# A seventeenth place for expert weights, with the tenants of its region moved

## The reference

```python
x = x + gt1 * (merged @ w_out[l])
h = rms_norm(x, norm2_g[l]) * (1.0 + sc2) + sh2
x = x + gt2 * hier_moe(h, ...)
return rms_norm(x, final_norm_g)
# hier_moe, for each of 4 groups of 8 experts:
hid = silu(einsum('td,edf->tef', hf, w1[gi])) * einsum('td,edf->tef', hf, w3[gi])
out = out + einsum('tef,efd->td', hid * combine[:, gi, :, None], w2[gi])
```

## Time and profile before

| | us |
|---|---|
| median of three runs | 686.97 |
| lowest, highest | 686.06, 691.97 |
| the profiled execution | 687.41 |
| its span, first to last instruction | 685.6 |

### The profile page before, as it was taken

The page is one execution under the profiler, slowest core; times in us unless marked ns, Lnnn a source line. Parts: engine busy times, 40 slices in busy tenths (PEclk is TensorE's granted clock), DMA queues, the critical chain, the costliest instruction groups (busy, mean ns, idle before and its releaser), DMA issues.

```text
span 685.6 us, 12601 instructions
## 1 busy us (share of the span) xinstructions
PE 661.1 (96%) x5274; PEld 531.1 (77%) x5274; DVE 428.0 (62%) x723; ACT 267.3 (39%) x375; POOL 71.4 (10%) x70
## 2 busy tenths in 40 slices
PE   8999999999999999999999999999999999999893
PEld 7999999998777778999989997676666666665441
DVE  4756988987777789978999686735242122121226
ACT  3346655548773524347353324231232212121102
POOL 0001000000004524200000000001111111111111
PEclk9999999999999999999999999999999999999997
DMA  8997454455334433356999989989999999999992
GB/s 362 422 377 255 176 184 145 164 184 185 123 123 141 167 124 123 123 174 228 388 398 394 344 320 421 376 309 405 411 395 419 420 421 419 419 418 419 420 362 83
DMA packets 31194, 201.22 MB, mean 293 GB/s; under 512 B 5047, under 2 KB 5431, under 8 KB 7970
## 3 DMA queue, kind: packets, MB, share of 16 engines
q1 hardware_dynamic: 27378, 193.27, 72.1%
q0 software_dynamic: 3760, 7.14, 2.8%
HBM read 195.35 MB, written 10.75 MB: 301 GB/s over the span
## 4 chain that ended last, share of the span: by engine, by line
PE 77%; DMA 9%; DVE 8%; SPq 2%; ACT 2%; issue 2%; DVEq 0%; ACTq 0%
PE ps L1555 75%; DMA ring<-in_expert_pieces 4%; DMA r_v<-in_pieces 4%; DVE ring_rounded L928 3%; SPq L451 1%; PE ps L1699 1%; DVE r_ct L1193 1%; PE ps L1991 1%; DVE r_v L1193 1%; ACT ring_rounded L638 1%; DMA r_xs<-in_x_t 1%; DVE r_xs_rounded L1214 0%; DVE r_kq L1157 0%; SPq L471 0%; DVE r_kq L1151 0%
## 5 line engine op out<-in xcount | busy, mean ns | idle before, releaser
L928 DVE TENSOR_TENSOR ring_rounded<-ring,ring_rounded 128x2048 fp32r<-128x2048 f32 x60 | 136.5, 2290 | 20.2 <-ACT ring_rounded L638 19.7
L1555 PE MATMUL ps<-hT_rounded,ring_rounded 128*128 128x256 f32 x832 | 148.1, 284 | 1.1 <-ACT hT_rounded L652 1.1
L1555 PEld LDWEIGHTS ps<-hT_rounded,ring_rounded 128*128 128x128 f32 x832 | 127.9, 191 | 4.4 <-issue 3.3
L638 ACT CAST ring_rounded<-ring 128x2048 fp32r<-128x2048 f32 x60 | 113.8, 1903 | 30.7 <-PE ps L1555 27.6
L1555 PE MATMUL ps<-ring_rounded,hT_rounded 128*128 128x512 f32 x352 | 111.2, 393 | 0.9 <-DVE r_bt_rounded L1243 0.9
L1555 PE MATMUL ps<-x_sb_rounded,ring_rounded 128*128 128x256 f32 x416 | 94.9, 283 | 0.0
L1555 PEld LDWEIGHTS ps<-x_sb_rounded,ring_rounded 128*128 128x128 f32 x416 | 76.5, 191 | 0.7
L1555 PEld LDWEIGHTS ps<-ring_rounded,hT_rounded 128*128 128x128 f32 x352 | 65.0, 188 | 15.3 <-issue 1.7
L852 ACT ACTIVATE sq<-ps 128x128 f32<-128x128 f32 x32 | 8.9, 277 | 141.3 <-PE ps L1555 141.3
L1438 DVE TENSOR_TENSOR r_st<-ps,r_kq 128x512 f32<-128x512 f32 x32 | 22.1, 692 | 64.9 <-PE ps L1555 64.9
L597 POOL DMA_INDIRECT y_rows<-r_st,r_btm x29 | 28.5, 984 | 317.6 <-DVE r_st L1438 311.5
(11 more groups left out here) (333 smaller groups left out, 1002.0 us busy)
## 6 DMA issues: line engine op xcount, KB each, us to landing
ring<-in_pieces SPq DMA_DIRECT2D x62, 1024.0 KB, 5.0
ring<-in_expert_pieces SPq DMA_DIRECT2D x48, 1024.0 KB, 16.2
r_z<-in_expert_pieces SPq DMA_DIRECT2D x12, 1024.0 KB, 11.7
r_xs<-in_expert_pieces SPq DMA_DIRECT2D x12, 1024.0 KB, 13.0
r_v<-in_pieces SPq DMA_DIRECT2D x8, 1024.0 KB, 8.3
r_ct<-in_pieces SPq DMA_DIRECT2D x8, 1024.0 KB, 6.7
g_sb<-in_expert_pieces SPq DMA_DIRECT2D x6, 1024.0 KB, 13.1
r_st<-in_expert_pieces SPq DMA_DIRECT2D x6, 1024.0 KB, 13.0
```

Of the source, the lines that this page charges most:

```text
L638: nc.scalar.copy(high_of(p_), slot_of(p_)).then_inc(hi_ok, 1)
L928: nc.vector.tensor_tensor(low_of(p_), slot_of(p_), high_of(p_).bitcast(F32), ALU.subtract).then_inc(lo_ok, 1)
L1555: return nc.tensor.matmul(o, l, r, start=start, stop=stop)
```

## The change

`MOE_SLOTS` is 17. The seventeenth place (number 16) is all of `r_kq`. Piece 16 is loaded into it behind pieces 12 and 13, once all four products of the first residual are added (`x2_done`) and the gate's bias has landed. From there the order of places has one more member, so each later piece goes to the place that was free one piece earlier in the list. The tenants of the region move:

- `gt2_two` and `c_half` to the upper 1024 columns of `r_st`. SP loads the bias there behind piece 6, after the merged halves were taken; ScalarE waits for the fourth merged half before it writes `c_half`.
- the three work areas of the search to constants in `par` that nothing reads any more; the search runs after expert 2's output (it was expert 1's), its ranks after expert 3's (2's).
- `fng` to the place whose last piece is used first among the last: place 12, `r_bt`, free after expert 26. POOL loads it behind the scatter of expert 27 (it was 8).
- the pieces of the loop for further windows to places 11, 13 and 14 (they were 2, 3 and 4).

`s_wr` becomes the counter of place 16 too, with a new name.

```diff
-MOE_SLOTS = 16
+MOE_SLOTS = 17
...
+SPARE = [s_ for s_ in range(2, MOE_SLOTS) if max(j for j in range(3 * E) if MOE_SLOT[j] == s_) < 3 * EARLY_E]
+NORM_SLOT = min(SPARE, key=lambda s_: max(j for j in range(3 * E) if MOE_SLOT[j] == s_))
+NORM_FREE = max(j for j in range(3 * E) if MOE_SLOT[j] == NORM_SLOT) // 3
+X_SLOTS = [s_ for s_ in SPARE if s_ != NORM_SLOT][:3]
...
-        gt2_two = r_q[:, 0:CW]
-        c_half = r_q[:, CW:2 * CW].rearrange("p (k n) -> p k n", n=W)
+        gt2_two = r_st[:, 3072:3072 + CW]
+        c_half = r_st[:, 3072 + CW:4096].rearrange("p (k n) -> p k n", n=W)
...
-                     r_xs[:, 2048:4096]] + ring_slot[:6] + [r_bt[:], view(hT, "p k t -> p (k t)")] + ring_slot[6:]
+                     r_xs[:, 2048:4096]] + ring_slot[:6] + [r_bt[:], view(hT, "p k t -> p (k t)")] + ring_slot[6:] + [r_kq[:]]
...
-        fng = r_k[:, 0:D]
+        fng = moe_slots[NORM_SLOT][:, 0:D]
...
-        jt = r_k[:, 0:3 * JOBS * E].rearrange("p (a b) -> p a b", b=E)
...
+        of_job, tmp_j, tmp_k = (par[:, PAR[n][0]:PAR[n][0] + JOBS * E].rearrange("p (a b) -> p a b", b=E)
+                                for n in ("same", "after", "inch"))
...
+        moe_full = [sem(f"moe_full{i}") for i in range(MOE_SLOTS - len(EARLY) - 1)] + early_full + [s_wr_then_moe]
+        full_ahead = [0] * (MOE_SLOTS - len(EARLY) - 1) + [1] * len(EARLY) + [3]
...
-                    for h in range(2):
-                        sp.dma_start(gt2_two[h * W:(h + 1) * W], gate_bias[h].partition_broadcast(W)).then_inc(s_wr, 16)
...
             for n in range(6):
                 piece_used(sp, RING_FREED[n][1])
                 load_moe(6 + n)
+                if n == 0:
+                    sp.wait_ge(s_wr_then_moe, 16)
+                    for h in range(2):
+                        unit_taken(sp, ("ob", 1), h)
+                    for h in range(2):
+                        sp.dma_start(gt2_two[h * W:(h + 1) * W], gate_bias[h].partition_broadcast(W)).then_inc(s_wr_then_moe, 16)
...
             load_moe(13)
+            sp.wait_ge(x2_done, 2 * TT)
+            sp.wait_ge(s_wr_then_moe, 48)
+            load_moe(16)
...
-                if e == 8:
-                    pool.wait_ge(jobs_ok, 1)
+                if e == NORM_FREE + 1:
+                    for done in (up_read, up_full, down_full):
+                        pool.wait_ge(done, NORM_FREE + 1)
                     pool.dma_start(fng, final_norm_g.partition_broadcast(P)).then_inc(s_crow_fng, 16)
...
+            act.wait_ge(m_full, 4)
             nc.scalar.copy(c_half, over(col("c", 0, 8), W)).then_inc(c_done, 1)
...
-            dve.wait_ge(s_wr, 48)
+            dve.wait_ge(s_wr_then_moe, 16)
...
             dve.wait_ge(gate_read, len(GATE_ROWS))
+            dve.wait_ge(s_wr_then_moe, 48)
             nc.vector.tensor_tensor(gt2_two, ps[GATE_BANK][:], gt2_two, ALU.add).then_inc(gate_ok, 1)
...
-                if e == 1:
+                if e == 2:
                     extra_windows()
...
-                if e == 2:
+                if e == 3:
                     ranks_of_extra_windows()
```

More of the change, by code:

```diff
@@ L306, in trunk @@
         start_row_read, mod_ok, x_sqrt_crow = (sem(n) for n in "start_then_row_read mod_ok x_sqrt_then_c_rows".split())
-        moe_full = [sem(f"moe_full{i}") for i in range(MOE_SLOTS - len(EARLY))] + [
-            sem(f"early_then_moe_full{i}") for i in range(len(EARLY))]
-        early_full = moe_full[MOE_SLOTS - len(EARLY):]
+        early_full = [sem(f"early_then_moe_full{i}") for i in range(len(EARLY))]
         hi_ok, lo_ok, half_read, ob_read, ada_read, up_read, gate_read, gate_ok, h_full, h_hi, m_full, m_hi, ob_hi, oa_hi, h_lo = (
@@ L325, in trunk @@
         fin_sqrt, fin_scaled, out_ready = (sem(n) for n in "fin_sqrt fin_scaled out_ready".split())
-        s_xT, s_x, s_small, s_par, s_const, s_ones, s_wr, s_crow_fng, s_gate = (sem(n) for n in "s_xT s_x s_small s_par s_const s_ones s_wr s_crow_fng s_gate".split())
+        s_xT, s_x, s_small, s_par, s_const, s_ones, s_wr_then_moe, s_crow_fng, s_gate = (sem(n) for n in "s_xT s_x s_small s_par s_const s_ones s_wr_then_moe s_crow_fng s_gate".split())
+        moe_full = [sem(f"moe_full{i}") for i in range(MOE_SLOTS - len(EARLY) - 1)] + early_full + [s_wr_then_moe]
+        full_ahead = [0] * (MOE_SLOTS - len(EARLY) - 1) + [1] * len(EARLY) + [3]
         s_pool = sem("s_pool_chain")
@@ L422, in moe_loaded @@
         def moe_loaded(eng, j):
-            eng.wait_ge(moe_full[MOE_SLOT[j]], 16 * (moe_turn(j) + 1 + (MOE_SLOT[j] >= MOE_SLOTS - len(EARLY))))
+            eng.wait_ge(moe_full[MOE_SLOT[j]], 16 * (moe_turn(j) + 1 + full_ahead[MOE_SLOT[j]]))
         def col(name, i=0, n=1):
@@ L482, in _ @@
                         unit_taken(sp, ("oa", 1), h)
-                    sp.dma_start(r_btm[:, 0:KD * 36 + 36], router_w).then_inc(s_wr, 16)
+                    sp.dma_start(r_btm[:, 0:KD * 36 + 36], router_w).then_inc(s_wr_then_moe, 16)
                     load_moe(3)
@@ L541, in _ @@
                     for h in range(3):
-                        sp.dma_start(moe_slots[2 + h], expert_pieces[e * 3 + h]).then_inc(x_loaded, 16)
+                        sp.dma_start(moe_slots[X_SLOTS[h]], expert_pieces[e * 3 + h]).then_inc(x_loaded, 16)
                     sp.wait_ge(x_added, j)
@@ L1366, in _ @@
             nth = over(count0[:, 0:JOBS], E)
-            of_job, tmp_j, tmp_k = (jt[:, i * JOBS:(i + 1) * JOBS] for i in range(3))
             def extra_windows():
@@ L2065, in _ @@
                     pe.wait_ge(x_taken, j)
-                    up([up_half(2 + r) for r in range(2)], lambda r: r or pe.wait_ge(x_loaded, j * 48), ps[0], x_rows, up_read, x_up)
+                    up([up_half(X_SLOTS[r]) for r in range(2)], lambda r: r or pe.wait_ge(x_loaded, j * 48), ps[0], x_rows, up_read, x_up)
                     pe.wait_ge(x_hid, j)
@@ L2069, in _ @@
                     pe.wait_ge(x_back, j)
-                    down(down_w(4), hidT[:, 0], ps[2], x_down)
+                    down(down_w(X_SLOTS[2]), hidT[:, 0], ps[2], x_down)
                     pe.wait_ge(x_weighted, j * 2)
```

## The result

| | before | after |
|---|---|---|
| median, us (14 runs each) | 687.03 | 682.51 |
| lowest, highest | 685.64, 691.97 | 681.55, 685.61 |
| profiled execution | 687.41 | 682.08 |

The ratio is 0.9939, with a 95% interval of 0.9926 to 0.9952: 4.2 us (3.3 to 5.1) faster. The forecast was 683.7 with a range of 682.5 to 686.1. The median lies inside by 0.01 us, which is luck as far as the range goes: the interval of the ratio reaches to both sides of that edge. The change of 0.6% is under the 1% that was called no change.

What follows compares the result with a forecast made beforehand. TensorE was taken to bound the kernel, waiting for expert weights near the end. TensorE's gain of 3.8 us less 0.2 for late reads gave -3.6 us: 683.7 us, range 682.5 to 686.1.

Steps and rivals of the forecast that it cites:

- The place: Expert weight stream: piece 16 fills unused transfer time from 444 to 460 us, so later pieces land 2.5 us earlier.
- The norm's row: Final norm's broadcast, moved behind expert 27's scatter: pieces awaited from 625 to 648 us come another 1.25 us earlier.
- TensorE's waits: End of expert stage: 4.06 us lost waiting for weights; 3.8 us gained, 0.3 us of waiting left.
- The search: Search for experts with over 64 rows, one expert later: TensorE 0.5 us earlier in mid stage, costed at nothing.
- The end: POOL's reads of scattered rows overlap the last weights 1.3 us more; 0.2 us loss taken, 1.3 upper bound.
- The other tenants: Gate bias, copies, search work areas and extra-window slots at new addresses: hidden, 0, at most 0.1 us either way.
- more gain: Expert stage: a fuller queue moves bytes better, waits vanish, the search's 0.5 us counts: -4.6, 682.8 us; chance 0.13.
- the gap does not take the piece: From 444 to 460 us other pieces are pushed back, only the norm's row gains: -1.3, 686.1 us; chance 0.09.
- the reads cost the full 1.3 us: Kernel's end: last weights and four reads collide for all 1.3 us: -2.5, 684.9 us; chance 0.15.
- nothing is visible: Whole kernel: an unseen wait eats the gain, time stays 687.4 us; chance 0.05.
- the slower case: POOL's queue: the norm's row takes 28.3 us and delays the last scatter: +10 us, 697 us; chance 0.03.

Runs made afterwards that it cites:

- run 7: Kernel before with the norm's row behind expert 27's scatter and the search one expert later: ratio 0.9976, median 685.54 us.
- control: The kernel before, run once more unchanged: ratio 1.0001, median 686.85 us.
- run 4: Kernel before with only the search and its ranks one expert later: ratio 1.0003, median 686.20 us.
- run 5: Changed kernel with the search back behind expert 1's output and its ranks behind expert 2's: ratio 0.9949 to the kernel before, median 683.33 us.
- run 2: Kernel before with only the gate's bias issued later, behind piece 6: ratio 1.0004, median 686.66 us.
- run 6: Changed kernel without the seventeenth place, all else as changed: ratio 0.9975 to the kernel before, median 685.32 us.
- changed_again: The changed kernel measured again, on another chip: ratio 0.9945 to the kernel before, median 682.50 us.
- runs 1 and 3: 1: kernel before, unchanged, 1.0001. 3: kernel before with only the norm's row moved behind expert 27's scatter, 0.9998.
- run 10: Kernel before, 16 places, pieces issued in TensorE's reading order: ratio 1.0055 with the end order wrong (the 4.51 us wait), 0.9971 with it corrected.

## Why the prediction was right, and where it was off

**The place: right.** Piece 16 went where it was forecast, and the stretch from 444 to 460 us took its bytes. The piece behind which TensorE waited last landed 1.95 us earlier in the changed kernel (643.11) than with the row alone (645.06), where 2.5 was forecast; by the means of the three groups of profiles in run 7 it is 2.2. By time the place is worth 2.1 to 2.5 us, with about 1.5 us to either side.

**The norm's row: right in its trace, uncertain in size.** 1.38 us by the landing, 1.31 by D, forecast 1.25; 1.3 by the means in run 7. The twelve timed runs of the row alone show 0 (about 1 us to either side). Both together: 646.44 to 643.11 is 3.33 us against the control, 3.75 was forecast. In the queue of POOL the row held nothing up.

**TensorE's waits: the mechanism was right, the size is that of an execution.** I read 4.06 us from one profile and took 3.8 of it as gained. From that profile to the one after it is 4.28 - 0.35 = 3.93; from the control, 2.94 - 0.35 = 2.59. The 0.3 us that I left was 0.35 in one profile and 0 in the other.

**The search: this step failed.** I costed it at nothing, since "who comes earlier to a stream that sets the end waits there longer". Alone it is so (run 4: C -0.62, D +0.60). But the same prediction had let the stream come 3.75 us earlier, up to 0.3 us short of TensorE without waits. In the changed kernel the stream set almost nothing any more (D 0.35 and 0), so there was nothing left to give the 0.6 us back to; run 5's profile bears this out, its times are too coarse for it. The sentence was true of the kernel before and was used for the kernel after. The size forecast for that case, 0.5, was nearly right (0.61).

**The end: right.** 0.2 us was taken for the late reads; E grew by 0.30 in the profile after, and by 0 in the second one.

**The other tenants: right,** nothing (run 2, and run 6 beside run 7).

**The sum.** From the control: D 2.59, C 0.61, E -0.30, together 2.9 us; the profiles are 3.03 us apart. From the first trace of before: 3.93 + 0.61 - 0.30, and 1.15 of B, which no part of the change touches, together 5.4 us; the two profiles are 5.33 apart (687.41, 682.08). The medians lie 4.5 apart, the ratio says 4.2. Forecast were 3.6. Counted from the first trace of before, from which the forecast was made, D and E give these 3.6 (3.93 - 0.30), and the 0.6 of the search makes the 4.2. Counted from the control the same terms come to 2.9 only, and 1.3 us of the 4.2 has no term. So that the sum meets the ratio is in part luck: by how much D shrinks depends on which execution before is taken. The case that came nearest is "more gain" (682.8 us): its condition that a fuller queue moves bytes better did not show (the place moved the stream by about 2.2 us), but its outcome did, waits gone and the search counted.

**The other cases.** That the gap does not take the piece is excluded by the landing at 643.11, that the reads cost the full 1.3 us by E, that nothing is visible by the ratio, and the slower case by the row's landing after 10.4 us, under the 18 us that it needed.

## What to carry to other kernels

Price an edit against the bound that is left once the other edits of the same change have worked, not against today's: a part that is worth nothing alone can count once another part has moved that bound. Read a wait of a few microseconds from more than one execution before building a sum on it. And where places are the limit, look at the order of issue too: an issuer that waits for the place freed last holds the ones behind it.

## What the runs showed of the hardware

**The same program loses time at fixed places in some executions.** Four of the fourteen profiles (A) have a stretch near 61 to 65 us at a lower granted clock, which costs 1.5 us. Of the run without the place:

```profile
60.00:66.00 6.00, 6.00 (x40) 6.00 (x40) 5.91 (x12) 5.49 (x6) 0.36 (x1) 0.72 0.95 332
```

In the control the clock is 1.00 there. TensorE shows no wait ahead of it in either; what it does just before, from 57.5 to 61.2 us, is 32 matmuls of 48 columns. Five of the fourteen profiles lose 1.1 to 2.3 us before 414 us (B) behind a later transfer of rows. B does not depend on the edits: of two profiles of one kernel, one has it and the other not (before and control, after and changed_again). A lies nearly 300 us ahead of the first load of an expert piece, so the edits have no visible way to it, but no kernel was profiled both with it and without it. Three of the four profiles were taken on one chip, which also gave one without it.

**The transfers take as long with 17 places as with 16.** The piece that lands last in time for TensorE took 27.54 us before, 27.68 and 27.70 in runs 1 and 3, and 27.94 after, though it was issued up to 6 us earlier. From about 610 us on, an issue holds SP for 2.1 to 2.3 us, nearly the time that a piece takes to move. SP's timeline after:

```profile
613.00 2.13 SPq L456 DMA_DIRECT2D r_st<-in_expert_pieces  x1
615.17 2.15 SPq L456 DMA_DIRECT2D r_xs<-in_expert_pieces  x1
617.37 2.30 SPq L456 DMA_DIRECT2D g_sb<-in_expert_pieces  x1
```

28 us at 2.5 us a piece are some 11 pieces on the way, fewer than there are places. From 613 us on SP issues without a pause between two of them. Earlier, SP pauses between its bunches in both kernels (after, one issue ends at 582.88 and the next starts at 588.30; an issue at 595.01 takes only 0.33 us), so there it is a place that it waits for. My reading is that at the end a full queue, and not a missing place, holds the next issue, and that the seventeenth place does its work early in the stage, by bringing one piece forward (the stretch from 444 to 460 us). No run separated the two.

**Behind a long wait TensorE ran at half its clock.** Behind the wait of 4.51 us in run 10 the granted clock was 0.50, and the product and the hidden layer behind it took 7.5 us in all (655.27 to 662.74 by the next row's start) where the changed kernel needs 5.3 (648.76 to 654.08). A wait of 0.80 us did not lower it. The stretch around that wait, in the control:

```profile
641.00:646.00 5.00, 3.77 (x25) 1.63 (x24) 2.72 (x9) 0.08 (x1) 0.98 (x1) 1.00 1.02 418
```
